# Handling the last two expert pairs by one-hot products, and dividing the closing sums and norm of a hybrid decoder step among VectorE, ScalarE and GpSimd

## What is computed

```python
w = e_w / jnp.sum(e_w, axis=-1, keepdims=True) * g_w
combine = jnp.einsum('nk,nke->ne', w, jax.nn.one_hot(expert_id, N_EXPERTS, dtype=f32))
for e in range(N_EXPERTS):
    h = jax.nn.silu(xt @ lp['w_e_gate'][e]) * (xt @ lp['w_e_up'][e])
    y = y + combine[:, e:e + 1] * (h @ lp['w_e_down'][e])
...
x = x + hier_moe(rmsnorm(x, lp['norm2_g']), lp)
y_prompt = rmsnorm(xp, final_norm_g)
```

## Time and profile before

| | |
|---|---|
| median of 3 runs | 805.71 us (805.52 to 807.05) |
| the profiled execution's own time | 806.09 us |
| its span (first to last instruction) | 804.3 us |
| PE, DVE, ACT, POOL busy | 758.0, 392.3, 244.2, 74.8 us |
| HBM read and written | 176.17 MB and 21.41 MB |

### The profile page before, as it was taken

One profiled execution on the slowest core, in us unless ns is written; L12 is line 12 of the kernel. 1 busy time (PEld: TensorE's weight loads), 2 busy tenths in 40 slices (PEclk: granted clock), 3 DMA queues, 4 the chain that ended last, 5 costly groups with the idle time before them and its releaser, 6 DMA issues.

```text
span 804.3 us, 12111 instructions
## 1 busy us (share of the span) xinstructions
PE 758.0 (94%) x4993; PEld 579.4 (72%) x4993; DVE 392.3 (49%) x734; ACT 244.2 (30%) x429; POOL 74.8 (9%) x104
## 2 busy tenths in 40 slices
PE   8999999999999999999999999999999997778875
PEld 6889999999998766789999989886333332323332
DVE  3599828994632757466244367546121121113237
ACT  1552333213473534552243252112111111100113
POOL 0100022001003010100000010011112211111100
PEclk9999999999999999999999999999999999999998
DMA  9668135623335454210241388269999999999986
GB/s 343 238 190 324 63 109 81 150 77 155 98 133 211 184 215 152 105 53 2 105 161 64 158 325 333 79 268 350 412 421 424 421 421 424 421 422 428 420 304 236
DMA packets 38731, 190.62 MB, mean 237 GB/s; under 512 B 5994, under 2 KB 7546, under 8 KB 22968
## 3 DMA queue, kind: packets, MB, share of 16 engines
q1 hardware_dynamic: 24288, 148.22, 46.7%
q0 software_dynamic: 11200, 34.98, 13.0%
q10 hardware_dynamic: 3184, 6.60, 2.2%
HBM read 176.17 MB, written 21.41 MB: 246 GB/s over the span
## 4 chain that ended last, share of the span: by engine, by line
PE 79%; DMA 11%; ACT 5%; DVE 3%; issue 1%; ACTq 0%; SPq 0%; DVEq 0%
PE ps L611 75%; DMA sb<-in_wexp 10%; PE ps L622 4%; ACT sr L1408 1%; ACT sb L1492 1%; DMA sb<-in_xT 1%; ACT sb L1421 1%; ACT sb L1293 1%; DVE sb L2421 0%; DVE sb L2063 0%; DVE sb L2028 0%; DVE sb L2500 0%; DVE sb L2049 0%; DVE sr L2001 0%; ACT sb L1437 0%
## 5 line engine op out<-in xcount | busy, mean ns | idle before, releaser
L611 PE MATMUL ps<-sb 128*64 128x512 f32 (+16 forms) x2216 | 385.0, 432 | 32.3 <-DMA sb<-in_wexp 21.1
L611 PEld LDWEIGHTS ps<-sb 128*64 128x64 f32 (+6 forms) x2216 | 219.4, 157 | 170.9 <-issue 133.5
L611 PE MATMUL ps<-sr 128*128 128x288 f32 (+2 forms) x2372 | 336.9, 302 | 4.2 <-DVE sr L2455 2.4
L611 PEld LDWEIGHTS ps<-sr 128*128 128x128 f32 x2372 | 320.2, 188 | 14.9 <-issue 8.1
L622 PEld LDWEIGHTS ps<-sb 128*128 128x128 f32 (+3 forms) x405 | 41.8, 140 | 30.0 <-issue 26.5
L2396 DVE SCALAR_TENSOR_TENSOR sb<-sb,ps 128x256 f32<-128x256 f32 x16 | 6.7, 421 | 112.0 <-ACT sb L1660 112.0
L622 PE MATMUL ps<-sb 128*128 128x128 f32 (+3 forms) x405 | 52.6, 269 | 1.5 <-DVE sb L2090 0.6
L2404 DVE COPY sb<-ps 128x1024 f32<-128x1024 f32 x15 | 18.4, 1225 | 61.4 <-PE ps L611 61.4
L2136 DVE TENSOR_TENSOR sr<-sb,sr 128x2048 fp32r<-128x2048 f32 (+1 forms) x15 | 34.7, 2324 | 27.4 <-ACT sr L1403 17.6
L1293 ACT ACTIVATE sb<-ps 128x576 f32<-128x576 f32 (+4 forms) x29 | 22.9, 789 | 70.4 <-PE ps L611 50.4
L2122 DVE SCALAR_TENSOR_TENSOR sb<-sb,ps 128x576 f32<-128x576 f32 x24 | 18.1, 753 | 53.3 <-PE ps L611 53.3
(11 more groups left out here) (275 smaller groups left out, 484.5 us busy)
## 6 DMA issues: line engine op xcount, KB each, us to landing
sb<-in_wexp SPq DMA_DIRECT2D x91, 1024.0 KB, 23.5
sb<-in_wstream SPq DMA_DIRECT2D x33, 1024.0 KB, 5.1
expert_rows<-sb ACTq DMA_DIRECT2D x1, 4608.0 KB, 21.3
sb<-in_mkT POOLq DMA_DIRECT2D x8, 512.0 KB, 9.7
sb<-in_mv POOLq DMA_DIRECT2D x8, 512.0 KB, 6.3
sb<-expert_rows SPq DMA_DIRECT2D x8, 512.0 KB, 8.1
sb<-in_wexp SPq DMA_DIRECT2D x5, 768.0 KB
sb<-in_x SPq DMA_DIRECT2D x4, 512.0 KB, 14.3
```

The lines of the kernel that those rows point to most:

```text
L611: return signed(nc.tensor.matmul(*a, **kw))
```

## The change

Pair 14 now goes the way of pair 15: no copy and no scatter; two halves by ACT (`high_rows`), low parts by DVE (`low_rows`), one-hot products by PE. All that this needs exists twice (`L_HI`, `L_LO`, `L_SEL`, `L_W`). `weigh_slots` runs at DVE's steps 11 and 13 (before: once, at step 12), `slot_weights` at PE's steps 12 and 14 (before: 13).

SP may ask for the result rows once pair 13 has been scattered and gate and up of pair 14 are through PE. Before, it waited for the scatter of pair 14 and for PE's down product of pair 14. The loads stand in the same queue behind the last weights and the gain, and their order is tiles 0, 3, 1, 2, 4.

The closing sums are dealt out anew. Only tile 2 keeps `own_rows` and `first_choice` on PE; `own_rows(2)` moves ahead of the last `gate_up`. Tiles 0, 3 and 4 get h + w0 * y0 (`add_first`) and + w1 * y1 (`add_second`) on DVE, into the row buffer, and then PE's sum from PSUM (`combine`). In tile 1 ACT multiplies both row buffers by their weights, POOL adds them to h (two `tensor_tensor` of 128x1024), and DVE adds PE's sum. In tiles 0 and 1 DVE only inverts the root, ACT multiplies h by it (`Copy` with a scale), and POOL multiplies by the gain. Stores of tiles 0 and 1 wait for POOL. DVE makes both low parts of pair 15 before its first sums, and three of its sums stand before its branch. PE's closing products (`sums`) stand in a branch body of their own, which runs when there is no overflow. The slots of the overflow chunks change with the new buffers; in the runs here nothing uses them.

```diff
-PE_TILES = {2: 0, 3: 3, 4: 2}
-PICKED = {0: 2, 1: 1, **PE_TILES}
-L_HI, L_LO, L_SEL, L_W = M_YO + 1024, M_XGT, M_XG + 1024, R_SS + 13
+PE_TILES = {2: 0}
+PICKED = {0: 2, 1: 1, 2: 0, 3: 3, 4: 2}
+LAST = (NPAIR - 2, NPAIR - 1)
+L_HI, L_LO = (dict(zip(LAST, places)) for places in ((O_A + 12544, M_YO + 1024), (O_A + 13568, M_XGT)))
+L_SEL, L_W = (dict(zip(LAST, places)) for places in ((O_X, M_XG + 1024), (R_SS + 5, R_SS + 13)))
+
+def copies(i):
+    return i + 1 if i < LAST[0] else max(LAST[0], i)
+
+def sent(i):
+    return i // 2 - (i > LAST[0] and i % 2 == 0)
-                for t in range(TT):
+                for t in (0, 3, 1, 2, 4):
...
-            sp.wait_ge(y_sent[0], 16 * (NPAIR // 2))
-            sp.wait_ge(y_sent[1], 16 * (NPAIR // 2 - 1))
-            sp.wait_ge(ew_used, CHUNK_AT["d", NPAIR - 2, 0, 1] + 1)
+            for k in range(2):
+                sp.wait_ge(y_sent[k], 16 * (NPAIR // 2 - 1))
+            sp.wait_ge(ew_used, CHUNK_AT["gu", NPAIR - 2, 1, 1] + 1)
             load_results()
...
-                sp.wait_ge(y_done, t + 1)
+                sp.wait_ge(*((gained, t + 2) if t < 2 else (y_done, t + 1)))
...
+            def picked(j, t, half, start=False, stop=False):
+                for k, y in enumerate((L_HI[j], L_LO[j])):
+                    last = mm(pat(PICKED[t], half * 512, (1, 512)), r32(L_SEL[j] + WTOK[t], 128), r32(y + half * 512, 512),
+                              start=(start and k == 0), stop=(stop and k == 1))
+                return last
...
-                if i == NPAIR - 3:
-                    slot_weights()
+                if i == NPAIR - 4:
+                    slot_weights(1)
+                if i == NPAIR - 2:
+                    slot_weights(3)
+                if last:
+                    own_rows(2)
                 gate_up(i, 1)
                 if last:
-                    own_rows(2)
+                    pe.wait_ge(y_lo, 2)
+                    for half in range(2):
+                        picked(LAST[0], 2, half)
                     turn_hidden(i)
                     return
                 turn_rows(i + 1)
...
+                for t in range(2):
+                    for half in range(2):
+                        picked(LAST[0], t, half, start=True)
...
+            def sums():
+                pe.wait_ge(y_lo, 3)
+                for t in range(3):
+                    for half in range(2):
+                        if t == 0 and half:
+                            pe.wait_ge(y_lo, 4)
+                        last = picked(LAST[1], t, half, stop=(t < 2))
+                    if t < 2:
+                        last.then_inc(more_ps, 1)
+                pe.wait_ge(diag_w, 1)
+                first_choice(2)
+                for half in range(2):
+                    picked(LAST[0], 3, half, start=True)
+                    last = picked(LAST[1], 3, half, stop=True)
+                last.then_inc(more_ps, 1)
+                pe.wait_ge(y_sum, 1)
+                for half in range(2):
+                    picked(LAST[0], 4, half, start=True)
+                    last = picked(LAST[1], 4, half, stop=True)
+                last.then_inc(more_ps, 1)
+            many, left = overflow(pe), list(owed)
+            with pe.If(many < 1):
+                sums()
+            with pe.If(many > 0):
+                owed[:] = left
                 own_rows(2, start=False)
...
-            for half in range(2):
-                pe.wait_ge(y_lo, half + 1)
-                for t in range(3):
-                    last = picked(t, half, start=(t < 2))
-                    if half and t < 2:
-                        last.then_inc(more_ps, 1)
-            own_rows(3)
-            for half in range(2):
-                picked(3, half, start=False)
-            pe.wait_ge(diag_w, 1)
-            first_choice(2)
-            pe.wait_ge(y_sum, 1)
-            own_rows(4)
-            for half in range(2):
-                picked(4, half, start=False)
-            first_choice(3)
-            first_choice(4)
+                sums()
...
+            def high_rows(j):
+                act.wait_ge(slot_oh, 4 if j == LAST[0] else 6)
+                for half in range(2):
+                    act.wait_ge(*((y_ps, j + 1) if half else (y_half, j - LAST[0] + 1)))
+                    fn(r32(L_HI[j] + half * 512, 512), pat(3, half * 512, (1, 512)), ACT.Copy, scale=at(L_W[j], (1, 1)))\
+                        .then_inc(y_hi, 1)
...
+                    if i == LAST[1]:
+                        high_rows(LAST[0])
...
+            high_rows(LAST[1])
+            act.wait_ge(ld_row[1], 48)
+            for k, w in enumerate((R_W0, R_W1)):
+                rows_1 = at(A_WG[1] + k * D, (1, D), pn=WROWS[1])
+                fn(rows_1, rows_1, ACT.Copy, scale=at(w + 1, (1, 1), pn=WROWS[1])).then_inc(scaled, 1)
...
+                if t in (1, 2):
+                    h = at(H_AT[t - 1], (1, D), pn=WROWS[t - 1])
+                    act.wait_ge(y_done, t)
+                    fn(h, h, ACT.Copy, scale=at(R_SS + 7 + t, (1, 1), pn=WROWS[t - 1])).then_inc(scaled, 1)
...
+            def low_rows(j):
+                for half in range(2):
+                    dve.wait_ge(y_hi, 2 * (j - LAST[0]) + half + 1)
+                    v.scalar_tensor_tensor(r32(L_LO[j] + half * 512, 512), pat(3, half * 512, (1, 512)), at(L_W[j], (1, 1)),
+                                           r32(L_HI[j] + half * 512, 512).bitcast(F32), ALU.mult, ALU.subtract).then_inc(y_lo, 1)
+            def add_first(t, rows_landed):
+                R = WROWS[t]
+                dve.wait_ge(ld_row[t], rows_landed)
+                op(v.scalar_tensor_tensor(at(A_WG[t], (1, D), pn=R), at(A_WG[t], (1, D), pn=R), at(R_W0 + t, (1, 1), pn=R),
+                                          at(H_AT[t], (1, D), pn=R), ALU.mult, ALU.add))
+            def add_second(t):
+                R = WROWS[t]
+                op(v.scalar_tensor_tensor(at(A_WG[t], (1, D), pn=R), at(A_WG[t] + D, (1, D), pn=R), at(R_W1 + t, (1, 1), pn=R),
+                                          at(A_WG[t], (1, D), pn=R), ALU.mult, ALU.add))
             def pairs(i0, i1):
...
+                    if i == NPAIR - 5:
+                        weigh_slots(LAST[0])
                     if i == NPAIR - 4:
                         weight_diagonals()
-                        weigh_slots()
+                    if i == NPAIR - 3:
+                        pick_weight(LAST[0])
+                        weigh_slots(LAST[1])
                     if i == NPAIR - 2:
-                        pick_slots()
-                result(i1 - 2)
+                        pick_tokens(LAST[0])
+                        pick_weight(LAST[1])
+                        pick_tokens(LAST[1])
+                if i1 == NPAIR:
+                    low_rows(LAST[0])
+                else:
+                    result(i1 - 2)
                 hidden(i1 - 1)
+            def sum_rows(rows_landed):
+                add_first(0, rows_landed)
+                add_second(0)
+                add_first(3, rows_landed)
+                c.settle()
             pairs(0, NPAIR)
-            for half in range(2):
-                dve.wait_ge(y_hi, half + 1)
-                v.scalar_tensor_tensor(r32(L_LO + half * 512, 512), pat(3, half * 512, (1, 512)), at(L_W, (1, 1)),
-                                       r32(L_HI + half * 512, 512).bitcast(F32), ALU.mult, ALU.subtract).then_inc(y_lo, 1)
+            low_rows(LAST[1])
+            sum_rows(48)
+            dve.sem_inc(added, 1)
             main, c = c, Chain(dve, over_step)
             with dve.If(overflow(dve) > 0):
...
+                if t not in PE_TILES:
+                    dve.wait_ge(more_ps, t + 1)
+                    c.do(v.tensor_tensor(h, pat(PICKED[t], 0, (1, D), pn=R), at(A_WG[t], (1, D), pn=R), ALU.add), y_sum)
+                    return
                 dve.wait_ge(ld_row[t], 48 if t < TT - 1 else 64)
-                if t not in PE_TILES:
-                    op(v.scalar_tensor_tensor(h, at(A_WG[t], (1, D), pn=R), at(R_W0 + t, (1, 1), pn=R), h, ALU.mult, ALU.add))
-                    op(v.scalar_tensor_tensor(h, at(A_WG[t] + D, (1, D), pn=R), at(R_W1 + t, (1, 1), pn=R), h, ALU.mult, ALU.add))
-                    dve.wait_ge(more_ps, t + 1)
-                    c.do(v.tensor_tensor(h, pat(PICKED[t], 0, (1, D), pn=R), h, ALU.add), y_sum)
-                    return
                 dve.wait_ge(more_ps, t + 1)
                 rest = pat(PE_TILES[t], 0, (1, D), pn=R)
                 c.do(v.scalar_tensor_tensor(h, at(A_WG[t] + D, (1, D), pn=R), at(R_W1 + t, (1, 1), pn=R), rest,
...
-                if t == 0:
+                if t < 2:
+                    c.do(v.reciprocal(ss, ss), y_done)
+                    return
+                if t == 2:
                     dve.wait_ge(ld["gf"], 16)
                 op(v.reciprocal(ss, ss))
                 c.do(v.scalar_tensor_tensor(h, h, ss, at(M_GF, (1, D), pn=R), ALU.mult, ALU.mult), y_done)
```

(37 more changed lines are left out.)

128 lines of the change are left out of this document (64 added, 64 removed).

## The result

| | kernel before, run beside it | changed kernel |
|---|---|---|
| median (lowest to highest) | 806.97 us of 6 (805.52 to 811.18) | 814.98 us of 6 (813.21 to 815.56) |
| the profiled execution's span | 804.3 us | 813.8 us |
| its own time | 806.09 us | 815.56 us |

The ratio is 1.008, with a 95% interval from 1.0055 to 1.0106: slower, by 0.8%, clear of no change but well under 2%. On the 805.71 us of the runs shown ahead it makes 812.2, against 811.9 forecast. The size is less sure than that: 6.4 us by the ratio (4.4 to 8.5 by its interval), 8.0 us between the two medians of the table, 9.5 us between the spans of the two traces, where 6.2 were forecast. The profiled execution of the changed kernel is the longest of its runs; that of the kernel before, 806.09 us, lies in the lower half of the range of its runs. What follows explains the traces' 9.5.

A forecast was written before the change was run, and what follows sets the result against it. The weights' stream bounds the kernel until 768.65 us, so only the last 35.7 us can change. Won 0.8, POOL's lock +6.1, stores +0.9: +6.2 us, span 810.5, median 811.9; range 805.0 to 813.5, the forecast's own 808.5 to 813.5.

The forecast's parts named there:

- Part 1: Row loads asked for sooner, behind the weights in the queue: last weights not delayed, gain at most 1.5 us.
- rival C: Row loads take DMA time from the last weights, so the last down product waits: +1 to +4 us; 0.06 with rival B.
- Part 2: Path from last gate/up product to low parts, without own_rows(2) before the transpose: 0.3 us won, bounds 0 and 0.5.
- Part 3: PE's closing products take 11 to 15 us beside DVE's sums; PE leaves the path, its 13.3 us no longer bind.
- Part 4: DVE alone from low parts until combine(1) ends: 10.8 us, so 790.6, with 0.25 for the branch, at most 1.5.
- Part 5: ACT's roots and scalings after combine(1) take 9.85 us; last gain product ends at 800.45, 0.8 us sooner.
- Part 6: POOL's four products lock out DVE operations with two SBUF operands: 4.3 us to combine(1), 1.8 later, 6.1 together.
- the alternative sum at the end of part 6: Without the port lock between POOL and DVE, the sum of Part 5 would stand: last gain product at 800.45.
- Part 7: Final stores: tiles 2 and 3 wait for tile 1 from POOL, four stores follow each other, 0.9 us more.
- Part 8: Earlier steps: PE's second wait for slot weights, about 747, counted zero under the weights' stream; up to 2.7 us if uncovered.
- rival B: PE's second stall, at step 14, reaches the last gate/up product: up to 2.7 us; chance 0.06 together with rival C.
- the prediction's own sign of B or C: PE starting the last gate/up product later than 769 would show rival B or rival C and the forecast wrong.

The follow-up runs named there:

- e7: Kernel before, with only own_rows(2) ahead of the last gate/up product and PE's closing products in their own branch body; 806.72 us, ratio 0.9977.
- e8: e7 with PE doing tile 4's own_rows and one-hot products ahead of first_choice(2); 804.71 us, ratio 0.9971 to the kernel before.
- e1: Changed kernel, with SP asking for the ten result-row loads only once the last down weights have landed; 812.67 us, ratio 1.0062.
- e6: Changed kernel without POOL's products, rows ordered 3, 1, 0, 2, 4, tile 0's loads held until the last weights landed; 813.85 us, ratio 1.0073.
- e4: Changed kernel with tile 0's rows loaded last instead of first; one run, 819.87 us.
- e2: Changed kernel with POOL's four products and ACT's four scalings given back to DVE; 813.84 us, ratio 1.0081.
- e5: Changed kernel with tile 0's two row loads made 128 partitions wide, twice the bytes, tile 0's results wrong; one run, 810.25 us.
- e3: Changed kernel with the edits of e1 and e2 together; 811.85 us, ratio 1.0058.

## Why the prediction was right, and where its steps were not

The sign and the range were forecast, and one of the two causes: the closing sums, with POOL's lock in them. The other, about half of the traces' loss, was taken for unlikely. That the time by the ratio (812.2) falls so close to the 811.9 is luck: against the forecast's own steps the low parts are 5.5 us later than its 779.8, from there to the last gain product it is 23.9 instead of 26.7, 2.8 less, and the end is 4.6 instead of 4.0. The first two errors cancel by half, and the traces still lie 3.3 us above the forecast.

- **Part 1 failed, and with it rival C's price.** "So the last weights aren't delayed" was concluded from the gain's landing (23.6 us, like the weights before it). That shows the order of *issue* is kept; it doesn't show that a transfer behind leaves one ahead of it alone. The gain is a full-width load, tile 0's rows are not. Rival C named the mechanism (+1 to +4) with a few hundredths of chance; it is what happened: the wait is 3.07 us, and with the clock that it cost, 4.8, more than its upper end. A row for it stood in the trace of before, not used: the window from 778 to 780 with share 0.98 at 225 GB/s.
- **Part 2 was right**: 0.30 us shorter from the last gate/up product to the copy of the transposes, as forecast.
- **Part 3 was half right.** PE left the path and DVE waited for none of its products. Its work went to DVE for that. e7 and e8 show that with PE's share left as it was the gap at the branch can be had alone, without that price: 0.9 us that are surely PE's, up to 2.0 with the earlier rows.
- **Part 4's branch was mis-sized.** It took 1.31 us on DVE, in all seven traces with a branch between DVE's sums (the change, e1 to e6), not ACT's 0.25; the forecast had 1.5 as its bound. In e8, where it stands ahead of the first sum as in the kernel before, it took 0.40.
- **Part 5 held as far as it can be read**: from `combine(1)` to ACT's last root it is 7.7 us, 8.2 forecast.
- **Part 6 had the right mechanism and the wrong size.** The lock is there, and by it DVE's operations with two SBUF operands took 3.87 us more in all, 1.59 up to `combine(1)` (4.3 forecast) and 2.28 behind it. The second pair delays the end by less than it blocks: ACT's last root ends at 806.11, and before the last gain product ended 1.5 us behind that root, so about 1.6 are net (1.8 forecast). The first was too high because POOL waits as well: its products took 2.73, 3.20 and 3.30 beside DVE against 2.33 to 2.39 alone (e4), and of two that collide, the one that started first ran its normal time: `add_first(3)` started at 787.84 and took 1.29, though POOL's product had begun at 788.60 by the trace. The branch and `combine(0)` covered part of the rest. The landing of tile 1's rows, 780.7 by the forecast, was wrong too: ACT got them at 787.36, behind the same slow stretch. The Trainium skill, SBUF — State Buffer, in the reading notes under its diagram of ports, has it as a lock that the first to start keeps; the runs now agree on both sides, and the alternative sum at the end of part 6, without a lock, fell.
- **What POOL costs is not what it blocks.** The forecast charged the change with 6.1 us for the lock. e2 shows that giving POOL's work back to DVE costs more (0.6) than the lock did, as far as the last gain product: four operations, 4 x 1.28 = 5.1 us, against 3.87. The lock made the offload nearly worthless. The 2.8 us between low parts and last gain product add up so: for tiles 3 and 4 DVE took over four sums from PE, and gave as many operations to POOL and ACT, so that its own work, each operation at its length when alone, is as long as before (18.4 against 18.6 us). What came is the lock, 3.87, and the branch between sums, 1.31; what went are 2.1 us of DVE's waits for rows, PE and ACT (2.76 before, 0.66 after); small overlaps are the rest. A run with PE's share kept and POOL's offload alone wasn't made, so which of the two moves is at fault isn't separated.
- **Part 7**: four stores behind POOL's tile 1, 0.9 forecast, 1.5 measured. The median landing of a full store rose from 2.6 to 3.9 us.
- **Part 8 was right.** PE waited for the second slot weights at 747.91, 0.79 us, and stood for weights 0.79 at 758.62 and 1.37 at 763.65 behind it. The cover held; rival B didn't occur. The last gate/up product started at 769.41, later than 769, and so the prediction's own sign of B or C showed. It was a poor sign: over the eight experiments the same product starts between 767.84 and 770.12, which points to the spread of the weights' stream, and what C meant showed at the down product instead.

## What to carry to other kernels

A transfer that is queued behind another is not thereby harmless to it: look for windows in which the DMA share is 1 and the rate is half of the usual, see which transfers run in them, and keep narrow ones away from whatever the next wait needs. A lock between two engines is priced against what the work costs without the second engine, not against zero. And once a wait is removed, ask at once what the engine that gained runs into: in e7's trace the gain was lost to the next operand, and exchanging two blocks of products took that wait away.

## What was not expected of the hardware

- In the windows with loads into 64 partitions the change moved 178 to 207 GB/s with the 16 DMA engines fully busy; with loads into 128 it was 406 to 426 (e5, same place in the program). The Trainium skill, SBUF — State Buffer, section on the DMA port swizzle, has a reason for it: partitions 0 to 63 reach only 8 of the 16 ports, with an asymptote of about 218 GB/s. The change's windows agree; single windows of e2 and e6 reach 229 to 254, and a window can't be split into narrow and full loads. That such loads also delay the weights ahead of them in the same queue (3.07 us here) the runs show. How the pieces collide inside the engines is open.
- The last down product of 16 matmuls took 3.65 us after 0.47 us of idling (e1, e3, e4, e5, e6) and 5.35 after 2.73 (e2) and 3.55 (the change), with the granted clock at 0.50 in the window behind. A wait of PE so costs about 1.7 us on top of itself here.
- A branch between DVE's sums costs it 1.31 us, and one ahead of them 0.40 (e8). PE, when it jumps past the rare body, stands 2.39 us; when its closing products are the body that it runs, they start 0.03 us after its last product (e7).
